# The low parts of the weights: every fourth chunk on GpSimd instead of VectorE

## What is computed

```python
def first_block(x, ...):
    proj = jnp.einsum('bsd,de->bse', rmsnorm(x, g_attn[l]), w_in[l])
    ...
    x = x + jnp.einsum('bse,ed->bsd', mixed, w_out[l])
    u = jax.nn.relu(jnp.einsum('bsd,df->bsf', rmsnorm(x, g_mlp[l]), w_up[l]))
    x = x + jnp.einsum('bsf,fd->bsd', u * u, w_down[l])
    return rmsnorm(x, g_final)
def second_block(x, ...):
    proj = _rmsnorm(h, attn_norm_g[l]) @ w_in[l]
    ...
    h = h + mix @ w_out[l]
    h = h + _peer(_rmsnorm(h, ffn_norm_g[l]), peer_w_query[l], peer_sub_keys[l], peer_u[l], peer_v[l])
    return _rmsnorm(h, final_norm_g)
```

## Time and profile before

| | us |
|---|---|
| median of 3 executions (3730.56 to 3732.28) | 3732.21 |
| the profiled execution | 3739.92 |
| its span, first to last instruction | 3738.1 |
| TensorE busy in the span | 3473.3 |
| VectorE busy | 2038.4 |
| ScalarE busy | 1478.3 |
| GpSimd busy | 211.4 |
| mean granted TensorE clock | 0.958 |

### The profile page before, as it was taken

How to read it: one execution, slowest core, us unless ns; L and a number is a source line. 1 busy time by engine, 2 the same in 40 slices (tenths; PEclk the granted TensorE clock), 3 DMA queues, 4 the chain that set the end, 5 groups by cost and what they waited for, 6 DMA issues and landing times.

```text
span 3738.1 us, 41259 instructions
## 1 busy us (share of the span) xinstructions
PE 3473.3 (93%) x15882; PEld 2831.9 (76%) x15882; DVE 2038.4 (55%) x2084; ACT 1478.3 (40%) x1309; POOL 211.4 (6%) x292
## 2 busy tenths in 40 slices
PE   7998899999999999964889758999999999999998
PEld 5886778888888878853868647888888888888886
DVE  3433555555555644366455996555555555555555
ACT  4335443444444443323234345333333333333333
POOL 0000100000000000031700052000000000000000
PEclk8997999999999999885989889999999999999999
DMA  6551255555555455400025336555555555555553
GB/s 238 190 188 59 81 180 181 187 182 180 186 184 186 174 201 183 155 0 1 1 94 188 136 90 189 199 198 195 194 199 191 197 195 192 199 192 192 198 195 129
DMA packets 120303, 607.43 MB, mean 162 GB/s; under 512 B 11552, under 2 KB 44704, under 8 KB 50976
## 3 DMA queue, kind: packets, MB, share of 16 engines
q1 hardware_dynamic: 82576, 571.74, 43.4%
q10 hardware_dynamic: 37648, 34.61, 3.2%
HBM read 587.43 MB, written 18.87 MB: 162 GB/s over the span
## 4 chain that ended last, share of the span: by engine, by line
PE 44%; DVE 6%; issue 1%; DMA 0%; ACT 0%; POOL 0%; DVEq 0%; ACTq 0%; POOLq 0%
PE pj L239 14%; PE pj L240 14%; PE pj L241 14%; DVE hotA L1587 1%; DVE lo L228 1%; PE pt L340 1%; PE pj L1239 1%; DVE hotB L1591 1%; DVE idx L1505 0%; DVE pos L1505 0%; DVE vals L1503 0%; PE pt L1255 0%; PE pj L1255 0%; DVE best L1503 0%; PE pm L1631 0%
## 5 line engine op out<-in xcount | busy, mean ns | idle before, releaser
L228 DVE TENSOR_TENSOR lo<-raw,hi 128x2048 fp32r<-128x2048 f32 x536 | 1227.6, 2291 | 1219.4 <-ACT hi L224 1218.2
L224 ACT ACTIVATE hi<-raw 128x2048 fp32r<-128x2048 f32 x536 | 1022.3, 1914 | 1260.3 <-PE pj L241 1247.6
L239 PE MATMUL pj<-hi,xh 128*128 128x512 f32 x2752 | 1095.1, 398 | 24.2 <-DVE lo L228 24.2
L240 PE MATMUL pj<-lo,xh 128*128 128x512 f32 x2752 | 1091.9, 397 | 0.0
L241 PE MATMUL pj<-hi,xl 128*128 128x512 f32 x2752 | 1091.4, 397 | 0.0
L239 PEld LDWEIGHTS pj<-hi,xh 128*128 128x128 f32 x2752 | 519.5, 189 | 150.2 <-issue 19.5
L241 PEld LDWEIGHTS pj<-hi,xl 128*128 128x128 f32 x2752 | 519.2, 189 | 126.1
L240 PEld LDWEIGHTS pj<-lo,xh 128*128 128x128 f32 x2752 | 519.6, 189 | 124.7
L239 PE MATMUL pj<-hi,coef_h 128*128 128x512 f32 x1536 | 611.8, 398 | 0.0
L240 PE MATMUL pj<-lo,coef_h 128*128 128x512 f32 x1536 | 607.2, 395 | 0.0
L241 PE MATMUL pj<-hi,coef_l 128*128 128x512 f32 x1536 | 607.0, 395 | 0.0
(11 more groups left out here) (343 smaller groups left out, 1880.0 us busy)
## 6 DMA issues: line engine op xcount, KB each, us to landing
raw<-w_peer SPq DMA_DIRECT2D x256, 1024.0 KB, 4.8
raw<-w_mlp SPq DMA_DIRECT2D x128, 1024.0 KB, 4.9
raw<-w_in SPq DMA_DIRECT2D x104, 1024.0 KB, 4.9
raw<-w_out SPq DMA_DIRECT2D x32, 1024.0 KB, 4.9
raw<-w_q SPq DMA_DIRECT2D x16, 1024.0 KB, 4.9
gates_scratch<-stage ACTq DMA_DIRECT2D x8, 2048.0 KB, 8.9
gate_e<-gates_scratch ACTq DMA_DIRECT2D x32, 512.0 KB, 3.5
resid<-x SPq DMA_DIRECT2D x4, 512.0 KB, 7.0
```

Source lines behind the costliest of these rows:

```text
L224: nc.scalar.activation(hi[:, j, :], raw[:, j, :], ACT.Copy).then_inc(hi_ready, 1)
L228: nc.vector.tensor_tensor(lo[:, j, :], raw[:, j, :], hi[:, j, :].bitcast(F32), ALU.subtract).then_inc(lo_ready, 1)
L239: nc.tensor.matmul(pair[:, t, :], sh[:, k0 + k, tok], hi[:, j, cols], start=begin, stop=False)
L240: nc.tensor.matmul(pair[:, t, :], sh[:, k0 + k, tok], lo[:, j, cols], start=False, stop=False)
```

## The change

GpSimd makes the low part of slot 3, VectorE those of slots 0, 1 and 2. The subtraction is the same. It has a semaphore of its own, `lo3_ready`, which counts quads, while `lo_ready` now counts three per quad; TensorE and SyncE wait for the one or the other by the slot. GpSimd's program gets four loops, each of one subtraction per quad: for `w_in` ahead of the attention, for `w_out` to `w_in2` ahead of HGRN, for `w_out2` to the first PEER quad ahead of the gates, and for the other 63 PEER quads behind them.

```diff
-        lo_ready = sem("lo_ready")
+        lo_ready, lo3_ready = sem("lo_ready"), sem("lo3_ready")
...
         def make_lo(dve, q, j):
+            if j == SLOTS - 1:
+                return
             dve.wait_ge(hi_ready, q * SLOTS + j + 1)
             nc.vector.tensor_tensor(lo[:, j, :], raw[:, j, :], hi[:, j, :].bitcast(F32),
                                     ALU.subtract).then_inc(lo_ready, 1)
+        def make_lo3(pool, q0, quads):
+
+            def body(i):
+                pool.wait_ge(hi_ready, i * SLOTS + (q0 * SLOTS + SLOTS))
+                nc.gpsimd.tensor_tensor(lo[:, SLOTS - 1, :], raw[:, SLOTS - 1, :], hi[:, SLOTS - 1, :].bitcast(F32),
+                                        ALU.subtract).then_inc(lo3_ready, 1)
+            turns(pool, quads, body)
+
+        def wait_lo(eng, q, j):
+            if j == SLOTS - 1:
+                eng.wait_ge(lo3_ready, q + 1)
+            else:
+                eng.wait_ge(lo_ready, q * (SLOTS - 1) + j + 1)
...
-            pe.wait_ge(lo_ready, q * SLOTS + j + 1)
+            wait_lo(pe, q, j)
...
-                            sp.wait_ge(lo_ready, (i + q0) * SLOTS + j - 3)
+                            wait_lo(sp, i + (q0 - 1), j)
...
         def _(pool):
+            make_lo3(pool, Q_IN1, G1)
             att1_pool(pool)
+            make_lo3(pool, Q_OUT1, Q_OUT2 - Q_OUT1)
             hgrn_pool(pool)
             delta_pool(pool)
+            make_lo3(pool, Q_OUT2, Q_PEER + 1 - Q_OUT2)
             gates_build_pool(pool)
+            make_lo3(pool, Q_PEER + 1, 2 * PEER_SB - 1)
```

## The result

| | before | after |
|---|---|---|
| median of the executions, us | 3732.58 (10, 3730.56 to 3734.72) | 3742.05 (10, 3740.89 to 3743.22) |
| the profiled execution, us | 3739.92 | 3740.89 |
| its span | 3738.1 | 3739.1 |
| VectorE busy | 2038.4 | 1759.6 |
| GpSimd busy | 211.4 | 830.5 |

The ratio is 1.0025, with a 95% interval of 1.0016 to 1.0035: the change costs 9.5 us. VectorE was relieved of 279 us and the kernel became slower.

The account below looks back on a forecast made before the run. The prediction took the weight stream as bound by TensorE; router -1.1, third w_in2 quad +5.8, clock +2.5 and second PEER quad +2.3 sum to +9.5 on 3732.2: 3741.7 us, own range 3738 to 3745, 8 in 10 3732 to 3746.

Parts of the forecast that it names:

- the 0.2% line: Whole kernel: about 7.5 us can be told from no change, which puts the line for slower at 3739.7 us.
- The price of the operation: One GpSimd subtraction takes 4.5 us against VectorE's 2.29; +2.3 us at each of two slot 3 chunks TensorE waits for.
- rival 3: GpSimd's operation is far longer than 4.5 us through the output format; at 7 us, 3752 us; chance 0.04.
- The steady stream costs nothing: Weight stream: slack falls from 12.6 to 10.3 us and covers GpSimd's longer subtraction, so cost zero.
- They don't meet: Weight stream: GpSimd ends 4.5 us after slot 3's hi; VectorE's next lo cannot begin before 5.6 us.
- Who gets the port: IN2 scaling and router: a waiting GpSimd operation gets between back-to-back two-input VectorE operations, holding the rest for 4.3 us.
- rival 1: Scaling and router: VectorE keeps its turn over consecutive operations; sum +2.4 us, 3734.6 us; chance 0.30.
- rival 2: As rival 1, but no clock fall at 1314.82 and less loss at 2300.63; -1.2 us, 3731.0 us; chance 0.06.
- The way from the scaling to TensorE: IN2: of the scaling's 4.3 us hold, 3.5 reach the third quad's slot 3; with 2.3, TensorE's chunk comes 5.8 later.
- The clock behind it: Third w_in2 quad: a TensorE wait of 7.9 us drops the clock to 1.2 GHz, +2.5 us (1.5 to 3).
- The router: Top-16 search: three subtractions less on VectorE, minus holds of its cand additions; -1.1 us of 4.7 possible.
- The span of 3747.6: Whole kernel: the profiled span of 3738.1 us was to become 3747.6 us.

Follow-up runs that it names:

- e9_twice: The changed kernel, but in 30 of the 32 MLP quads GpSimd does its subtraction twice, one after the other; 3742.36 us, ratio 1.0024.
- e10_four: The changed kernel, but in 30 MLP quads GpSimd does its subtraction four times; 4056.66 us, ratio 1.0867.
- e1_second: The changed kernel, but VectorE keeps slot 3 of the second w_in2 quad, the one behind the scaling; 3738.3 us, ratio 1.0016.
- e7_one: The kernel before, but GpSimd makes one single subtraction, slot 3 of the second w_in2 quad; 3738.7 us, ratio 1.0013.
- e8_write: The kernel before, but for slot 3 of the second w_in2 quad GpSimd writes zeros by memset, reading nothing; 3731.64 us, ratio 0.9994.
- e4_gate: The changed kernel, but in the search's three rounds GpSimd's subtraction waits until VectorE's two cand additions are done; 3738.53 us, ratio 1.0013.
- e2_both: The changed kernel, but VectorE keeps slot 3 of the second and third w_in2 quads; 3734.84 us, ratio 1.0005.
- e3_three: The changed kernel, but VectorE keeps slot 3 of the second and third w_in2 quads and of the second PEER quad; 3731.28 us, ratio 0.9994.
- e5_best: e3_three with the waits of e4_gate added; 3728.02 us, ratio 0.9985.
- e6_tail: e5_best, but GpSimd also makes slots 1 and 2 of the second PEER quad, the second behind the last cand additions; 3721.62 us, ratio 0.9967.

## Why the prediction was right

The median of 3742.05 stands beside the 3741.7 predicted, and the ratio's interval lies above 1 and reaches on both sides of the 0.2% line. Step by step:

- **The price of the operation.** 4.5 us from a slope over two shorter rows of GpSimd; measured 4.52 at the two chunks for which TensorE stands idle, 4.6 in the stream, and the output format costs nothing that shows (rival 3 is out). The sum has 2.3 us for what GpSimd takes longer, where 4.52 less 2.29 is 2.2. No run shows a slower hand-over from GpSimd to TensorE: the matmul starts 0.05 us behind the end of the lo from either engine. What the runs show is at the other end: GpSimd starts 0.08 us behind the end of the hi, VectorE 0.03.
- **The steady stream costs nothing.** Right for the time; e9_twice shows a margin of at least another 4.6 us, and e10_four that it is not without end. "They don't meet" was not quite right: 62 of the 402 subtractions that VectorE keeps took 2.35 to 2.46 us instead of 2.29, held by the end of GpSimd's. That they are off the path is what makes it free. That past the slack each quad pays was right in kind; the size that I expected for e10_four was too low by a factor of 2.8, since it counted neither the second contest nor the clock.
- **Who gets the port.** This was the choice on which the 7.1 us between the forecast and rival 1 hung, and it was made on two tenths of a microsecond. The scaling ended at 1279.90 in an execution that is 2.25 us ahead of before's at this place, which is 1282.15 on that clock; 1282.1 was forecast. e1_second takes the hold away, e7_one puts it alone into the old kernel, e8_write takes only the reading away. Rival 1, and rival 2 with it, fell at the first step.
- **The way from the scaling to TensorE.** Of 4.35 us, 3.5 were to arrive; the wait grew by 5.84 with 2.3 of it the longer subtraction, so 3.5. e1_second, with 3.58, and e7_one, with 3.56, show the same without the longer subtraction in the difference.
- **The clock behind it.** Forecast 2.5 from the one slow stretch in the profile of before; measured 2.59. That it is so close is luck. Behind the same 2.2 us wait the clock stayed up in before's profile, but cost 1.5 us behind e8_write's, where nothing holds the scaling either; and behind 8.0 us it cost only 1.5 in e4_gate's. In the medians 9.5 us less the waits' 7.55 (5.84 + 2.34 - 0.63) leaves 1.9 for the clock at both places.
- **The router.** The sign and the mechanism were right, the size 0.5 too favourable (-0.63 for -1.1). The holds were 4.42, 0.66 and 0.66 for 4.3, 0.6 and 0.6: that explains 0.2. The other 0.2 are the two reads directly behind their `cand` pair, 0.1 each, which the prediction put at nothing.
- **The span of 3747.6 was wrong**, by 8.5 us, with a right median. It took the profiled execution of before as the base of a profiled execution of after. But that execution was a long one, chiefly in HGRN and the delta rule, and what it had above the median does not come with the change. The sum belongs on the median, where it also was put.

What I would give other chances to now: the clock at waits of 2 to 3 us. The prediction took "it stayed at 1.00 behind 2.16 us" as a property of that wait. In e2_both, e3_three, e5_best and e8_write the same wait cost 1.5 us, in e6_tail nothing.

Open: in each place that I looked at, the operation that had been waiting got in between two of the other engine's; what decides when both have been waiting is not tested. HGRN and the delta rule are longer the more of their matmuls start at 1.2 GHz; why that number differs between executions is not settled either. It isn't the change: e4_gate has the change and 349 us like before, e8_write is without it and has 344 like after.

## What to carry to other kernels

Moving work from VectorE to GpSimd paid here only where VectorE ends last. Its price is the slower operation where something waits for it (2.3 us at each of two chunks), and, easier to overlook, what VectorE runs back to back, with two inputs in SBUF, at the moment when the moved operation becomes ready (3.5 us on the path at the scaling). Look for these places one by one: here three of 134 moved operations gave the whole loss, three in the search gave back most of what they saved, and the others were free. Where they collide, put GpSimd's operation behind the burst with a wait (4.0 us gained for three waits) or leave that one on VectorE; with both, and two more moved at the end of the search, the same idea gives 0.33% instead of costing 0.25%, some 2 of these 12 us by the clock.

## What the runs showed that I had not expected

- The clock falls at times behind a wait of 2.2 us. By profiled executions, e10_four apart: 2.2 us cost 0 (twice) or 1.5 us (four times), 3.0 to 3.2 us cost 0, 1.5 or 2.6, and 4.4 us and more always something, 1.5 to 2.8, with the 1.5 behind one of the longest, 8.0 us. So two kernels with the same waits can differ by some 4 us here, as much as an edit brings.
- The same instructions of HGRN and the delta rule take 342.4 to 349.4 us by execution, more than most of the differences looked for in this study.
- A GpSimd operation asked for too often does not only use up the slack: four that take 18.4 us alone took 23.3 beside VectorE, and the kernel lost 314 us.
